# The first RMSNorm chunk of a decoder layer: squares summed by TensorE instead of added up by VectorE first

## The reference

```
def rms_norm(x, w):
    xf = x.astype(jnp.float32)
    y = xf * lax.rsqrt(jnp.mean(xf * xf, axis=-1, keepdims=True) + EPS)
    return (y * w.astype(jnp.float32)).astype(x.dtype)

def mixer(xn, ...):
    proj = xn @ w_in
    a_val, a_gate, q, k, v, g, gate_a, gate_b = jnp.split(proj, IN_SPLITS, axis=-1)
    u = a_val * jax.nn.sigmoid(a_gate)
    ...
```

## Time and profile before

| | us |
|---|---|
| median of three runs | 1543.3 |
| the profiled execution | 1543.9 |
| its span, first to last instruction | 1542.0 |
| TensorE busy | 1486.9 (96%) |
| VectorE busy | 1025.2 (66%) |
| ScalarE busy | 652.0 (42%) |
| GpSimd busy | 845.4 (55%) |
| first TensorE matmul starts at | 8.09 |
| TensorE's continuous work starts at | 37.47 |

### The profile page before, as it was taken

The page is one execution under the profiler, slowest core; times in us unless marked ns, Lnnn a source line. Parts: engine busy times, 40 slices in busy tenths (PEclk is TensorE's granted clock), DMA queues, the critical chain, the costliest instruction groups (busy, mean ns, idle before and its releaser), DMA issues.

```text
span 1542.0 us, 28494 instructions
## 1 busy us (share of the span) xinstructions
PE 1486.9 (96%) x11410; PEld 1468.3 (95%) x11410; DVE 1025.2 (66%) x1265; ACT 652.0 (42%) x954; POOL 845.4 (55%) x564
## 2 busy tenths in 40 slices
PE   6999999989999999998999999999999999999995
PEld 5999999989999899997999999999999999999995
DVE  7897888678464853656732886666656756474846
ACT  6434433333444532253112665566556433332333
POOL 1467777777544572337348345555555555454555
PEclk9999999999999999999999999999999999999998
DMA  5112232331255328641143034557768575454634
GB/s 183 43 40 86 94 126 94 119 104 56 90 179 169 93 82 338 218 139 35 48 158 89 1 124 149 176 206 248 248 220 284 201 284 203 155 207 165 220 103 166
DMA packets 109931, 229.13 MB, mean 149 GB/s; under 512 B 8800, under 2 KB 20832, under 8 KB 108144
## 3 DMA queue, kind: packets, MB, share of 16 engines
q1 hardware_dynamic: 95136, 204.30, 38.4%
q10 hardware_dynamic: 14672, 23.09, 4.4%
HBM read 154.41 MB, written 72.95 MB: 147 GB/s over the span
## 4 chain that ended last, share of the span: by engine, by line
PE 81%; DVE 8%; ACT 4%; POOL 3%; issue 3%; DMA 1%; POOLq 0%; ACTq 0%; SPq 0%; DVEq 0%
PE ps L1425 38%; PE ps L1186 18%; PE ps L993 13%; PE ps L1351 3%; PE ps L1338 3%; PE ps L1114 1%; PE ps L1115 1%; PE ps L1118 1%; DVE v L2363 1%; DVE qk L2373 1%; DVE qk L2372 1%; DVE u_ext L2380 1%; DVE ro_l L2471 1%; DVE v L2467 1%; PE ps L1129 1%
## 5 line engine op out<-in xcount | busy, mean ns | idle before, releaser
L1425 PE MATMUL ps<-tx_h,w_h 128*128 128x258 f32 x960 | 271.6, 283 | 1.4 <-POOL w_l L962 0.9
L1425 PE MATMUL ps<-tx_l,w_h 128*128 128x258 f32 x960 | 271.3, 283 | 0.0
L1425 PE MATMUL ps<-tx_h,w_l 128*128 128x258 f32 x960 | 271.1, 282 | 0.0
L962 POOL TENSOR_TENSOR w_l<-raw,w_h 128x512 fp32r<-128x512 f32 x120 | 186.8, 1561 | 148.3 <-ACT w_h L1994 147.8
L1425 PE MATMUL ps<-fx_l,w_h 128*128 128x258 f32 x720 | 203.7, 283 | 0.0
L1425 PE MATMUL ps<-fx_h,w_h 128*128 128x258 f32 x720 | 203.6, 283 | 0.0
L1425 PE MATMUL ps<-fx_h,w_l 128*128 128x258 f32 x720 | 203.3, 282 | 0.0
L1425 PEld LDWEIGHTS ps<-tx_h,w_h 128*128 128x128 f32 x960 | 181.4, 189 | 1.8 <-POOL w_l L962 1.1
L1425 PEld LDWEIGHTS ps<-tx_l,w_h 128*128 128x128 f32 x960 | 181.3, 189 | 0.1
L1425 PEld LDWEIGHTS ps<-tx_h,w_l 128*128 128x128 f32 x960 | 181.2, 189 | 0.0
L2277 DVE SCALAR_TENSOR_TENSOR ps<-u_ext,wdw,ps 128x512 f32<-128x512 f32 x232 | 154.9, 749 | 0.1
(11 more groups left out here) (371 smaller groups left out, 4385.8 us busy)
## 6 DMA issues: line engine op xcount, KB each, us to landing
raw<-wseq_dram SPq DMA_DIRECT2D x264, 256.0 KB, 3.1
quad_scratch<-quad_h SPq DMA_DIRECT2D x16, 774.0 KB, 3.6
tx_h<-quad_scratch SPq DMA_DIRECT2D x12, 1032.0 KB, 10.6
tx_l<-hidden_scratch SPq DMA_DIRECT2D x12, 1032.0 KB, 13.0
gate_scratch<-gst SPq DMA_DIRECT2D x10, 1032.0 KB, 5.1
hidden_scratch<-hq_g SPq DMA_DIRECT2D x8, 1032.0 KB, 7.0
hidden_scratch<-stg_b SPq DMA_DIRECT2D x6, 1032.0 KB, 6.9
hq_g<-hidden_scratch SPq DMA_DIRECT2D x6, 1032.0 KB, 13.0
```

Of the source, the lines that this page charges most:

```text
L962: pool.tensor_tensor(lo, src, hi.bitcast(F32), ALU.subtract).then_inc(q_lo, 1)
L1425: out = pe.matmul(ps[:, 2 * n + s, 0:HC], RINGS[q % RING][wa][:, kk * P:(kk + 1) * P], OPS[x][xb][:, QK * kh + kk, at_:at_ + HC], start=(i ...
```

## The change

TensorE takes all eight squared tiles of chunk 0 itself, one float32 ones-matmul for each, accumulating in the same PSUM region. The four additions of VectorE on that chunk go away (two calls of `sq_add` in each of the two passes of the loop), and so does VectorE's wait for ScalarE's squares there. `x_one` now tells of VectorE's squares of pairs 1 and 3, and `x0_sq`, which VectorE used to wait for, now releases TensorE for pairs 0 and 2. The numbers that chunks 1 and 2 wait for on `x_one` stay the same.

```
             def x_stat(c, k, first, last):
 
-                if c < 2:
-                    pe.wait_ge(x_one, 2 * c + (2 if k else 1))
+                if c == 0:
+                    if k % 4 == 0:
+                        pe.wait_ge(x0_sq, k // 4 + 1)
+                    elif k % 4 == 2:
+                        pe.wait_ge(x_one, k // 4 + 1)
+                elif c == 1:
+                    pe.wait_ge(x_one, 3)
                 else:
                     pe.wait_ge(x_one, 4)
...
-            x_stat(0, 0, True, False)
-            x_stat(0, 4, False, True)
+            for k in range(KT):
+                x_stat(0, k, k == 0, k == KT - 1)
             x_stat(1, 0, True, False)
...
             for i in (1, 3):
                 dve.wait_ge(xa_in[i], 16)
-                step(dve.tensor_tensor(first[:, 2 * i:2 * i + 2], x_first[:, 2 * i:2 * i + 2],
-                                       x_first[:, 2 * i:2 * i + 2], ALU.mult))
-                dve.wait_ge(x0_sq, (i + 1) // 2)
-                step(sq_add(0, 2 * i - 2, 2))
-                sq_add(0, 2 * i - 2, 1).then_inc(x_one, 1)
+                dve.tensor_tensor(first[:, 2 * i:2 * i + 2], x_first[:, 2 * i:2 * i + 2],
+                                  x_first[:, 2 * i:2 * i + 2], ALU.mult).then_inc(x_one, 1)
```

## The result

| | before | changed |
|---|---|---|
| median, us (15 executions of each, side by side) | 1543.7 | 1547.79 |
| lowest and highest, us | 1542.8 to 1548.1 | 1545.4 to 1549.6 |
| ratio of the changed kernel to the one before | | 1.0023 (95%: 1.0015 to 1.0031) |
| first profiled execution, us | 1543.9 | 1548.14 |
| its span, us | 1542.0 | 1546.3 |

The forecast was 1544.4, the range 1542.7 to 1547.0. The time lies above the range: the sign of the centre was right, the size of the loss (1.1) was not. The page of the profile after shows the same work, with TensorE busy for 97% and VectorE 2 us less.

A forecast was written before the change was run, and what follows sets the result against it. The prediction took the start to be bound by the chain through VectorE's additions to chunk 0's statistic, and TensorE from 37.47 us on. A statistic 1.1 us later gave 1543.3 + 1.1 = 1544.4, range 1542.7 to 1547.0.

The forecast's parts named there:

- the sign of the centre: For the whole kernel, the central forecast was a loss: 1.1 us slower, from 1543.3 to 1544.4.
- What bounds the start: In the first 12 us, VectorE's four additions stand on the path; later work waits for chunk 0's statistic at about 11.77.
- VectorE's half sum allows no gain over 0.4 us: Chunk 0's scaling stands behind VectorE's half sum of chunk 1, so the path could gain only 12.96 - 12.57 = 0.4 us.
- The price of a statistic: TensorE's sixteen chunk 0 instructions start at 5.90, cost 0.573 us each at the lower clock, 0.29 at full, without late squares.
- The rise: TensorE's clock rises 4.25 us after its start at 5.90, between 2.8 and 5.7, making the statistic 1.1 us later.
- a wider spread of the changed kernel: Repeated runs of the changed kernel would spread more than the 0.7 us of the runs before.
- The second place: TensorE idles some 3 us before the projection matmuls near 16.4; a clock fall there adds 0.9 at worst, or nothing.
- so +1.1 goes on to 12.96 + 1.1 and from there unchanged: Everything behind chunk 0's statistic, from Ln and scaling on, shifts by 1.1 us to the end, with no later slack.
- a later clock dip comes or goes: Rival: a 1 us shift creates or removes a later half-clock stretch, up to 1.75 us; time 1542.6 or 1546.2; chance 0.15.

The follow-up runs named there:

- half the change: Against the kernel before, TensorE takes tiles 0 to 3 of chunk 0 directly while VectorE still adds tiles 4 to 7; ratio 1.0003.
- the warm start: The changed kernel with eleven matmuls of ones on TensorE ahead of its first statistic; ratio 1.0017 to the kernel before, +2.3 us.
- the fills: Matmuls of ones at the waits near 122 and 343 us: changed kernel 1.0013, kernel before 1.0003; kernel before with the first fill moved ahead of its wait 0.9983.
- the kernel before with a warm start: The kernel before with eleven matmuls of ones on TensorE ahead of its first statistic and nothing else; ratio 1.0010, +1.5 us.
- both pure delays: The kernel before with three or six in-place ScalarE copies of the chunk 0 statistic ahead of Ln; ratios 1.0011 and 1.0015.
- both bridges: The changed kernel with ten matmuls of ones behind `x_stat(1, 0)`, then with eight more ahead of chunk 1's first matmuls; ratios 1.0024 and 1.0021 to before.
- the bridge: The changed kernel with ten matmuls of ones behind `x_stat(1, 0)`, in TensorE's idle time of 14 to 17 us; ratio 1.0024 to the kernel before.

## Why the prediction was wrong

*What bounds the start: right.* The chain went through the additions, and with them gone it goes through the statistics. That VectorE's half sum allows no gain over 0.4 us is nearly right: half the change came out 0.6 ahead, the warm start 0.7.

*The price of a statistic: right.* 0.573 us apart at the lower clock, 0.289 at the full one, as worked out from the earlier trace rows; start at 5.94 instead of 5.90; no wait for a square.

*The rise: right as a range, low as a value.* Forecast 4.25 us after the start, between 2.8 and 5.7. Across the four changed traces the clock rose at 11.27, 10.56, 11.59 and 9.17, so 3.2 to 5.6 us after the start, and Ln came 1.7, 1.4, 1.8 and 0.7 later. Mean +1.4 where +1.1 stood. The Trainium skill says in "TensorE: Matmul & The Clock Gate", Part 1, that the moment of release shifts from run to run; these four moments agree. Its consequence, a wider spread of the changed kernel, is weakly borne out: the standard deviation is 1.1 us over its 35 executions and 0.8 over the 123 of before. From lowest to highest, in the fifteen of each, it is 4.1 us against 5.3 of before, where a single execution at 1548.1 makes half of it. Either way it is far more than the 0.7 of the three runs I was given.

*The second place: right in its outcome.* The clock fell behind the gap of 3 us, as one branch had it. The fall cost nothing: the eight instructions from 18.89 were done before ScalarE wanted them at 23.45.

```profile
23.45 0.50 ACT L1481 ACTIVATE ps<-ps,eps_b 128x344 f32<-128x344 f32 x1
```

(ScalarE's timeline; no idle time before it.)

*The step that failed: "so +1.1 goes on to 12.96 + 1.1 and from there unchanged", with the rival "a later clock dip comes or goes" at 0.15, half in each direction.* Behind 38 us the four pairs of traces differ by another 2.4 us, of which a stretch near 123 makes 0.9 and the late load 1.2. Two errors are in that step. First, the dips were taken to be as likely to go as to come, and to hang on tenths of a microsecond of gap, from one trace that turned out to be a cheap one: without the stretch near 123, which two of four traces of the same kernel have. Three runs 0.7 us apart had seemed to show that nothing varied; the 123 executions of before average 1544.3. There was one more dip to gain and little to lose. The size of the gap never decided it, as the earlier trace rows already showed: a fall lay beside a gap of 1.80 us and none behind 2.88. Second, the load near 650 stood nowhere in the account. The change was priced by the time of its instructions alone; that twelve more of them also move every later load of TensorE's code was put at nothing, without a reason.

How far this is shown: that half-clock stretches bind is (the fills). That the changed kernel has more of them is shown by the mean clock: 0.9893 over 34 executions against 0.9915 over 123. The difference is 0.0022 x 1545 = 3.4 us of clock, and one stretch takes 0.5 x 3.4 = 1.7 of it, so two stretches more. One is the free one at 18; about one is left that is paid for. The traces say the same: counted in lengths of 3.4 us, each changed one has six stretches, those of before have three, five, three and four. But the mean clock doesn't tell paid stretches from free ones: the kernel before with a warm start had 0.9882, the lowest of all, and was slower by 1.5 us only. That the paid one is the stretch at 123 rests on four traces against four.

*What stays open.* Why the clock falls more often behind a gap that is 2.9 us in every trace. Of the traces without fills, those of both pure delays, of both bridges, of half the change and of before with a warm start have the stretch too, and the changed kernel with a warm start doesn't, so neither the change nor the size of the shift decides it alone. And whether the late load goes when TensorE's code load is moved out of its way with nothing else altered: that experiment would turn the twenty traces into a proof, and it was not run.

## What to carry to other kernels

Before forecasting a microsecond from one trace, ask for several traces of the same kernel and list, for each, the stretches at half clock: a gap of some 3 us of idle TensorE is a place where the next execution may pay 1.2 to 1.4 us that this one did not. TensorE work near the start of a kernel, or behind an idle gap, is to be priced at the lower clock, where eight float32 statistics cost more than the four additions of an idle VectorE. Matmuls of ones that fill a gap pay if they stand ahead of the wait that makes it, end before the real work is released, and the next gap behind them does not grow. When instructions are added to an engine, look also at the `instruction` packets of its queue in the DMA view: a load of code that comes to lie inside a group of transfers on the path can cost more than the instructions themselves.

## What the runs showed of the hardware that I had not expected

- The same idle gap of 2.88 to 2.90 us was followed by full clock in two traces of one kernel and by half clock in the two others, and in one changed trace by 6.8 us of it.
- A TensorE that is early can lose what it gained: in its trace the bridge took a free stretch away, the wait behind it grew from 0.95 to 2.34 us, and a paid one followed.
- Eleven matmuls of ones from 1.1 us on raised the clock by 4.2 us in the changed kernel, and its statistics ran at full clock from 5.68 us. In the trace of the kernel before the same eleven, at the same time, didn't raise it by 6.1 us. A warm start of this length is not sure to work.
- TensorE's code arrives in packets of 16 KB, one for every 256 of its matmuls and loads. Where one started 3.3 to 6.0 us behind the issue of `v_bc`, among other transfers, that load took 8.9 to 9.4 us instead of 7.7 to 8.2.
- The granted clock of the profile reads 1.00 from 5.9 to 11.2 us of the changed kernel while the spacing of the instructions is that of half the clock; near the start it is the spacing that tells (the first change on record in that trace is the rise at 11.27).
